# Latent-attention branch: head projections in pairs, the rotary parts of four heads in one tile, and scores summed from two products

## The chip, the cores and the metric

The kernel runs on one core of a Trainium2 chip. The engines of the core work side by side and meet at semaphores: TensorE (PE; its loading of stationary weights is listed apart as PEld), VectorE (DVE), ScalarE (ACT), GpSimd (POOL) and SyncE (SP), which issues most transfers. The metric is the time of one execution on the device in microseconds (us); lower is better. Three runs of the kernel before gave a median of 3520.85 us (3520.58 to 3526.13).

## The reference, cut to what matters

Two blocks with three attention branches each are followed by further layers, over 512 tokens of width 1024. Only the latent branch (here "A") is touched by the change. It has 8 heads. A head's query has 64 plain dimensions and 32 that are turned by the rotary embedding; the 32 rotary dimensions of the key are shared by all heads:

```python
def mla_mixer(c_q, c_kv, k_rope, g_q, g_kv, w_uq, w_ukv):
    q = (rms_norm(c_q, g_q) @ w_uq).reshape(B, S, MLA_HEADS, MLA_NOPE_DIM + MLA_ROPE_DIM)
    kv = (rms_norm(c_kv, g_kv) @ w_ukv).reshape(B, S, MLA_HEADS, MLA_NOPE_DIM + MLA_V_DIM)
    q_nope = q[..., :MLA_NOPE_DIM]
    q_rope = apply_rope(q[..., MLA_NOPE_DIM:], cos[:, None], sin[:, None])
    k_nope, v = kv[..., :MLA_NOPE_DIM], kv[..., MLA_NOPE_DIM:]
    k_rope = apply_rope(k_rope, cos, sin)
    ...
        s = (jnp.einsum('bqhd,bkhd->bhqk', qn, k_nope) + jnp.einsum('bqhr,bkr->bhqk', qr, k_rope)) * scale
        p = jax.nn.softmax(s, axis=-1)
        return jnp.einsum('bhqk,bkhd->bqhd', p, v)
```

S is 512, the latent ranks are 256 (queries) and 128 (keys and values).

## The kernel before, in words

All activations lie feature-major: features on the 128 partitions, 512 tokens along the free dimension. A projection (`feature_major`) takes 128 columns of weights as the stationary operand and streams 512 tokens; every product is three matmuls of split operands (high by high, low by high, high by low; lines 2278 to 2280). The weights come through HBM as a packed stream of 532 units of 128x1024. SP loads a unit into a ring of three, ACT rounds it into `w_hi` (L1337), DVE takes the difference into `w_lo` (L1730), and PE waits for that before a unit's first use. `split_ahead` and `before` set at which place of the ACT and DVE programs the next unit is split: as soon as the slot of three units earlier is free by the program's order.

Per layer the attention goes through seven groups of four heads: C0, B0, B1, B2, A0, A1, C1. `n_dense` says how many projection steps a group has (A: 5). While PE does the first three of them, it also does what is left of the group before (`attend(..., m)`, m = 0, 1, 2), so that softmax latency is covered. A group's own main part then runs in steps of two heads and one tile of 128 queries ("pair"): V (values), S (scores), T (probabilities transposed by PE), O (output). T lags S by two pairs and O by three. A latent group has 8 pairs.

In a latent group before, each head has its own projection of keys `kA` (128 columns, of which DVE keeps 64: L2059) and of queries `qA` (96 columns, two ranks deep, evicted by ACT at L1357). The rotary part is turned over the whole 96-row tile of each head: PE multiplies by a signed permutation (`rotation`, L2431), DVE multiplies that by the sine (L1883), POOL multiplies the tile by the cosine (L1200), DVE adds (L1891). POOL also copies the shared rotary key `kr` under each head's key (L1233). A score is then one float32 matmul over 96 rows (L2488). DVE takes the negated row maximum (L1898), ACT the exponential (L1510). T is L2496 with evictions by DVE (L1996) and ACT (L1521); O is L2509 or L2519.

Two things run around the start of A0. The last part of B2 ends with `mix_dilations` on DVE (L1956 to L1970), which needs one exponential of ACT in its middle (L1526) and after which POOL does the mixing (L1244 to L1246). And ACT copies out `qA` of head 3 only behind that exponential. Around the start of A1, the outputs of B2 and A0 are transposed (`turned`, L2406) and split into halves: high by ACT (L1366), low by DVE (L1743).

PSUM has eight banks. During attention S, T, V and the projections go round six of them in the fixed order of the plan, O has the other two. `start_group` makes PE wait until the bank's last content has been read.

## Time and profile before

| what | value |
|---|---|
| median of three runs | 3520.85 us |
| profiled execution | 3523.32 us |
| its span, first to last instruction | 3521.2 us |
| mean granted TensorE clock | 0.981 |
| PE busy | 3416.2 us, 97% of the span |
| DVE busy | 1615.7 us, 46% |
| ACT busy | 1192.3 us, 34% |
| POOL busy | 357.4 us, 10% |

The span is what one execution took from its first to its last instruction. A busy share is an average over all stages. The granted clock is the share of full speed (2.4 GHz) at which TensorE was allowed to run; 0.5 is the lower level of 1.2 GHz. Matmuls overlap, so what one costs in a row of them is the distance between two starts and not its own duration. One float32 matmul shows up as two records, a 128-column transpose and an fp32r product as one.

### The profile page before, as it was taken

Reading aid. Unit: us, or ns where it says so; the run is one execution under the profiler, and the core shown is the slowest. Engines: PE = TensorE matmul, PEld = TensorE weight load, DVE = VectorE, ACT = ScalarE, POOL = GpSimd, SP = SyncE. Lnnn points to the kernel's source line nnn. Section 1 sums busy time; section 2 is a strip of 40 time slices with the busy share of each in tenths; the row PEclk is TensorE's granted clock in tenths of the full one; section 3 lists DMA queues with packets and bytes.
Section 4 is the critical chain, followed back from the end, with each engine's and each line's share of the span. In section 5 each row is a group of like instructions: output and inputs, shape, how many; then the busy total and the mean of one; then the engine's idle time right before and its main releaser. Section 6 shows DMA issues by size and latency. Waiting matters only on the chain.

```text
span 3521.2 us, 41468 instructions
## 1 busy us (share of the span) xinstructions
PE 3416.2 (97%) x17020; PEld 2828.2 (80%) x17020; DVE 1615.7 (46%) x2332; ACT 1192.3 (34%) x1936; POOL 357.4 (10%) x325
## 2 busy tenths in 40 slices
PE   7998999999999999999999999999999999999998
PEld 6786788788887767887888888888888887788887
DVE  4446444434344455444343454333533357764244
ACT  3333322322233333323322332222422236643222
POOL 2013000100011120000000010001300031130001
PEclk9999999999999999999999999999999999999999
DMA  4121122222222211222222222222222222222222
GB/s 148 43 84 36 41 90 96 90 96 98 99 96 75 73 48 36 70 97 90 96 96 96 96 99 79 89 81 78 75 99 94 98 78 72 86 89 93 94 99 74
DMA packets 82954, 296.51 MB, mean 84 GB/s; under 512 B 9584, under 2 KB 11856, under 8 KB 82640
## 3 DMA queue, kind: packets, MB, share of 16 engines
q1 hardware_dynamic: 80064, 284.89, 23.8%
q0 software_dynamic: 2704, 8.98, 0.8%
q8 instruction: 136, 2.23, 0.3%
q14 instruction: 50, 0.41, 0.0%
HBM read 290.66 MB, written 3.18 MB: 83 GB/s over the span
## 4 chain that ended last, share of the span: by engine, by line
PE 89%; DVE 5%; ACT 4%; issue 1%; POOL 1%; DMA 0%; SPq 0%; DVEq 0%; ACTq 0%; POOLq 0%
PE bank L2278 26%; PE bank L2280 26%; PE bank L2279 26%; PE bank L2519 3%; PE bank L2488 3%; PE bank L2496 2%; DVE w_lo L1730 1%; PE bank L2636 1%; ACT w_hi L1337 1%; ACT arena L1517 1%; PE bank L2431 1%; DVE arena L2188 1%; PE bank L2345 1%; PE bank L2624 0%; DVE h_lo L1832 0%
## 5 line engine op out<-in xcount | busy, mean ns | idle before, releaser
L1730 DVE TENSOR_TENSOR w_lo<-raw_ring,w_hi 128x1024 fp32r<-128x1024 f32 x532 | 679.2, 1277 | 1306.0 <-ACT w_hi L1337 1305.1
L2278 PE MATMUL bank<-h_hi,w_hi 128*128 128x512 f32 (+1 forms) x2752 | 1073.8, 390 | 46.2 <-DVE w_lo L1730 30.3
L2279 PE MATMUL bank<-h_lo,w_hi 128*128 128x512 f32 (+1 forms) x2752 | 1060.1, 385 | 0.0
L2280 PE MATMUL bank<-h_hi,w_lo 128*128 128x512 f32 (+1 forms) x2752 | 1059.5, 385 | 0.0
L1337 ACT ACTIVATE w_hi<-raw_ring 128x1024 fp32r<-128x1024 f32 x532 | 562.0, 1057 | 1134.1 <-PE bank L2280 1063.9
L2278 PEld LDWEIGHTS bank<-h_hi,w_hi 128*128 128x128 f32 x2752 | 523.3, 190 | 158.1 <-issue 37.6
L2280 PEld LDWEIGHTS bank<-h_hi,w_lo 128*128 128x128 f32 x2752 | 522.9, 190 | 103.6
L2279 PEld LDWEIGHTS bank<-h_lo,w_hi 128*128 128x128 f32 x2752 | 523.2, 190 | 102.8 <-issue 2.6
L2278 PE MATMUL bank<-act_hi,w_hi 128*128 128x512 f32 (+2 forms) x1352 | 516.0, 382 | 10.8 <-DVE act_lo L1743 7.7
L2279 PE MATMUL bank<-act_lo,w_hi 128*128 128x512 f32 (+2 forms) x1352 | 512.3, 379 | 0.0
L2280 PE MATMUL bank<-act_hi,w_lo 128*128 128x512 f32 (+2 forms) x1352 | 512.1, 379 | 0.0
L1357 ACT ACTIVATE arena<-bank 128x512 f32<-128x512 f32 (+2 forms) x252 | 146.4, 583 | 644.7 <-DVE bank L1777 435.6
L2278 PEld LDWEIGHTS bank<-act_hi,w_hi 128*128 128x128 f32 (+1 forms) x1352 | 254.1, 188 | 61.6 <-issue 8.2
L2280 PEld LDWEIGHTS bank<-act_hi,w_lo 128*128 128x128 f32 (+1 forms) x1352 | 254.3, 188 | 48.6
L2279 PEld LDWEIGHTS bank<-act_lo,w_hi 128*128 128x128 f32 (+1 forms) x1352 | 254.4, 188 | 47.6 <-issue 0.2
L1777 DVE TENSOR_TENSOR bank<-bank,rb 128x512 f32<-128x512 f32 x148 | 102.7, 695 | 169.7 <-PE bank L2280 168.5
L2278 PE MATMUL bank<-w_hi,h_hi 128*128 128x256 f32 x576 | 163.8, 284 | 0.0
L2280 PE MATMUL bank<-w_hi,h_lo 128*128 128x256 f32 x576 | 163.0, 283 | 0.0
L2279 PE MATMUL bank<-w_lo,h_hi 128*128 128x256 f32 x576 | 163.0, 283 | 0.0
L1120 POOL TENSOR_TENSOR arena<-arena 128x512 f32<-128x512 f32 x42 | 58.2, 1387 | 906.9 <-ACT arena L1376 906.0
L2488 PE MATMUL bank<-arena 64*128 64x128 f32 (+4 forms) x464 | 125.7, 520 | 14.7 <-DVE arena L1891 9.5
L2519 PEld LDWEIGHTS bank<-arena 128*128 128x128 f32 x928 | 115.5, 199 | 6.4 <-ACT arena L1521 3.2
(193 smaller groups left out, 2785.5 us busy)
## 6 DMA issues: line engine op xcount, KB each, us to landing
raw_ring<-weights SPq DMA_DIRECT2D x532, 512.0 KB, 3.3
arena<-rpb POOLq DMA_DIRECT2D x16, 320.0 KB, 4.5
xs<-x_t SPq DMA_DIRECT2D x4, 512.0 KB, 7.8
out_t<-xs SPq DMA_DIRECT2D x16, 128.0 KB, 1.8
arena<-block SPq DMA_DIRECT2D x1, 1024.0 KB, 12.0
arena<-o_nat POOLq DMA_DIRECT2D x2, 512.0 KB, 3.3
arena<-ret POOLq DMA_DIRECT2D x4, 256.0 KB, 3.0
o_nat<-arena POOLq DMA_DIRECT2D x2, 384.0 KB, 3.0
```

The costliest lines, as they stand in the source:

```text
L1120: ins = nc.gpsimd.tensor_tensor(tile(sq), tile(sq), tile(sq + k), ALU.add)
L1337: nc.scalar.activation(w_slot(w_hi, u), raw_slot(u), ACT.Copy).then_inc(w_hi_ready, 1)
L1357: nc.scalar.activation(dst, src, func, scale=scale).then_inc(gelu_freed if key[0] == "ly" else act_freed, 1)
L1517: nc.scalar.activation(probs[:, at], masked[:, at], ACT.Exp, scale=-1.0, bias=neg, accum_out=total).then_inc(probs_ready, 1)
L1730: nc.vector.tensor_tensor(w_slot(w_lo, u), raw_slot(u), f32(w_slot(w_hi, u)), ALU.subtract) \
L1777: nc.vector.tensor_tensor(b[:, :], b[:, :], rb[:, :], ALU.mult).then_inc(row_scaled, 1)
L2278: nc.tensor.matmul(out, lhs[0], rhs[0], start=first, stop=False)
L2279: nc.tensor.matmul(out, lhs[0], rhs[1], start=False, stop=False)
L2280: return nc.tensor.matmul(out, lhs[1], rhs[0], start=False, stop=last)
L2488: mm = nc.tensor.matmul(b[rows, at], q, k, start=True, stop=True)
L2496: mm = nc.tensor.transpose(tile_t(b, n), tile_t(tile(PB + u % PB_RING), n), c("ident"))
L2519: mm = nc.tensor.matmul(b[:, t * HEAD:(t + 1) * HEAD], tile_t(turned_probs, n), V[:, k0 + n, d], start=n == 0, stop=n == k1 - k0 - 1)
```

## The change

The weights are regrouped. For a group of four heads, `qr` is one projection whose 128 columns are the rotary parts of four heads; `kA` and `qA` are now projections of two heads each, 64 plain dimensions per head, side by side on 128 partitions. A latent group has 3 projection steps in place of 5. The rotary tile `Q[:, 2, :]` is turned once for all four heads (`n_rotated`). The rotary key's weight columns are repeated four times in the input projection, so that `kr` comes out on all 128 partitions, and POOL's copies fall away. A score is two float32 matmuls that accumulate in one bank: one over the head's 64 plain rows, one over its 32 rotary rows. The two heads of a pair take turns: plain, plain, rotary, rotary. The packed stream has 530 units.

```diff
-            c = cols(m * P, P) if m < 3 else cols(A_COLS - MLA_QK, MLA_QK)
+            c = cols(m * P, P) if m < 3 else cols(A_COLS - MLA_ROPE, MLA_ROPE) * GH
...
-            for i, h in enumerate(heads):
-                many(out, (l, "kA", g, i), ("w_ukv", l), range(1), cols(h * P, P))
-                many(out, (l, "qA", g, i), ("w_uq", l), range(2), cols(h * MLA_QK, MLA_QK))
+            many(out, (l, "qr", g), ("w_uq", l), range(2),
+                 [(h * MLA_QK + MLA_NOPE, (h + 1) * MLA_QK) for h in heads])
+            for i in range(2):
+                two = heads[2 * i:2 * i + 2]
+                many(out, (l, "kA", g, i), ("w_ukv", l), range(1), [(h * P, h * P + MLA_NOPE) for h in two])
+                many(out, (l, "qA", g, i), ("w_uq", l), range(2),
+                     [(h * MLA_QK, h * MLA_QK + MLA_NOPE) for h in two])
...
-    return 6 if turns_v(br, g) else 5
+    return 6 if turns_v(br, g) else 3 if br == "A" else 5
+def n_rotated(br):
+    return {"A": 1, "B": 4, "C": 0}[br]
...
-                pool.wait_ge(cos_done, nth_rope(l, "B", 2, 3))
-                wait_acc(pool, (l, "B", 2, "S", GH - 1))
-                for half in range(2):
-                    two = slice(2 * half, 2 * half + 2)
-                    one = kr[r, :].rearrange("p (o s) -> p o s", o=1).to_broadcast([MLA_ROPE, 2, S])
-                    nc.gpsimd.tensor_copy(K[r, two, :], one).then_inc(krope_done, 1)
-                    pool.wait_ge(krope_done, 2 * l + half + 1)
-                    for m in range(2 * half, 2 * half + 2):
-                        cosines("A", 0, m)
-                    pool.wait_ge(cos_done, nth_rope(l, "A", 0, 2 * half + 1))
+                cosines("A", 0, 0)
+                pool.wait_ge(cos_done, nth_rope(l, "A", 0, 0))
...
-                    before((l, "rot", "A", 0, LAG_O - 2))
+                    before((l, "qA", 0, 1))
...
-                        if br == "A" and m < GH:
-                            copy_out((l, "qA", g, m), Q[0:MLA_QK, m, :], rows=MLA_QK, scale=MLA_QK ** -0.5)
+                        if br == "A":
+                            copy_out((l, "qA", g, m - 1) if m else (l, "qr", g), Q[:, m - 1 if m else 2, :],
+                                     scale=MLA_QK ** -0.5)
...
-                            nc.vector.tensor_copy(K[0:MLA_NOPE, m, :], b[0:MLA_NOPE, :]).then_inc(dve_freed, 1)
+                            nc.vector.tensor_copy(K[:, m - 1, :], b[:, :]).then_inc(dve_freed, 1)
...
-                if br == "A":
-                    return slice(0, P), slice(0, S), tile_t(Q[0:MLA_QK, i, :], t), K[0:MLA_QK, i, :]
+                if br == "A" and n:
+                    r = slice(MLA_ROPE * i, MLA_ROPE * (i + 1))
+                    return slice(0, P), slice(0, S), tile_t(Q[r, 2, :], t), kr[r, :]
...
-                                pe.wait_ge(rope_done, nth_rope(l, br, g, i))
-                                pe.wait_ge(krope_done, 2 * l + 1 + i // 2)
+                                pe.wait_ge(rope_done, nth_rope(l, br, g, 0))
+                                pe.wait_ge(krope_sum, l + 1)
+                                wait_freed(pe, (l, "kA", g, i // 2))
+                                wait_freed(pe, (l, "qA", g, i // 2))
...
-                        parts = NT if strided(br, g) else 2 if (br, g, t) == ("B", 0, 0) else 1
+                        parts = NT if strided(br, g) else 2 if br == "A" or (br, g, t) == ("B", 0, 0) else 1
...
-                                mm = nc.tensor.matmul(b[rows, at], q, k, start=True, stop=True)
+                                mm = nc.tensor.matmul(b[rows, at], q, k, start=br != "A" or n == 0,
+                                                      stop=br != "A" or n == 1)
```

PE's program at the first two pairs of A0, before: the last two rotations, the values V, the scores of pair 0, V, the scores of pair 1 (a row is one matmul, banks numbered).

```order
L2431 MATMUL bank5<-arena,fixed_sb 96x512
L2431 MATMUL bank0<-arena,fixed_sb 96x512
...
L2280 MATMUL bank2<-w_hi,act_lo 128x256
L2488 MATMUL bank3<-arena 128x512
L2488 MATMUL bank4<-arena 128x512
L2278 MATMUL bank5<-w_hi,act_hi 128x256
...
L2280 MATMUL bank0<-w_hi,act_lo 128x256
L2488 MATMUL bank1<-arena 128x512
L2488 MATMUL bank2<-arena 128x512
```

The same place in the changed program, from the last output of B2 (L2508) on; `kr` marks the rotary part of a score.

```order
L2508 MATMUL bank6<-arena 128x64 x4
L2508 MATMUL bank7<-arena 128x64 x4
L2275 MATMUL bank1<-w_hi,act_hi 128x256
...
L2277 MATMUL bank2<-w_hi,act_lo 128x256
L2486 MATMUL bank3<-arena 128x512
L2486 MATMUL bank4<-arena 128x512
L2486 MATMUL bank3<-kr,arena 128x512
L2486 MATMUL bank4<-kr,arena 128x512
```

No rotation stands between the last outputs of B2 and the scores any more, and each score bank is written by two matmuls.

DVE's program at the same place, before: from the last outputs of B2 (L1939) through `mix_dilations` to the first row maximum of A0 (L1898).

```order
L1939 COPY arena<-bank7 128x4x64
L1956 TENSOR_TENSOR small<-small 128x16
...
L1970 TENSOR_TENSOR small<-small 128x16 x3
L2059 COPY arena<-bank3 64x512
L1730 TENSOR_TENSOR w_lo<-raw_ring,w_hi 128x1024
L1883 TENSOR_TENSOR cs<-bank5,arena 96x512
L1891 TENSOR_TENSOR arena<-arena,cs 96x512
L1883 TENSOR_TENSOR cs<-bank0,arena 96x512
L1891 TENSOR_TENSOR arena<-arena,cs 96x512 x2
L1898 TENSOR_REDUCE small<-bank3 128x1
```

The same in the changed program (L1938 are the outputs, L1955 to L1969 `mix_dilations`, L1890 the only rotary addition, L1897 the row maximum).

```order
L2057 COPY arena<-bank5 128x512
L1890 TENSOR_TENSOR arena<-arena,cs 128x512
L1938 COPY arena<-bank6 128x4x64
L1938 COPY arena<-bank7 128x4x64
L1955 TENSOR_TENSOR small<-small 128x16
...
L1969 TENSOR_TENSOR small<-small 128x16 x3
L1731 TENSOR_TENSOR w_lo<-raw_ring,w_hi 128x1024
L1897 TENSOR_REDUCE small<-bank3 128x1
```

The rotary addition has moved ahead of `mix_dilations`; behind it only one weight split is left before the first row maximum.

DVE's program at the start of A1 in the changed kernel: outputs of A0 (L1945), weight splits, low halves of the transposed outputs. Before, one split stood among the rotary work, and one before the last key copy.

```order
L1945 TENSOR_TENSOR arena<-bank7,small 128x4x64
L1731 TENSOR_TENSOR w_lo<-raw_ring,w_hi 128x1024 x2
L1744 TENSOR_TENSOR act_lo<-bank1,act_hi 128x512
L1744 TENSOR_TENSOR act_lo<-bank2,act_hi 128x512
L1744 TENSOR_TENSOR act_lo<-bank3,act_hi 128x512
L1744 TENSOR_TENSOR act_lo<-bank4,act_hi 128x512
```

The two splits now stand together, straight ahead of the four low halves.

## Rows read from the trace of the kernel before

**Rows 1.** The page: the chain that ended last, by engine.

```profile
PE 89%; DVE 5%; ACT 4%; issue 1%; POOL 1%; DMA 0%; SPq 0%; DVEq 0%; ACTq 0%; POOLq 0%
```

**Rows 2.** PE's waits: line, who released it, us in total, times, longest.

```profile
PE bank L2488 <- DVE arena L1891: 9.5, 2, 4.9
...
PE bank L2431 <- ACT arena L1357: 5.5, 4, 2.5
...
PE bank L2488 <- DVE act_lo L1743: 4.5, 4, 1.9
PE bank L2278 <- DVE cs L1883: 3.3, 4, 1.3
```

**Rows 3.** Stretches: start:end, length, busy times, PEclk, DMA share, GB/s.

```profile
287.24:295.71 8.47, 8.47 (x18) 4.35 (x19) 7.64 (x8) 3.42 (x10) 8.23 (x4) 0.69 0.03 10
344.15:353.18 9.03, 9.03 (x19) 4.53 (x19) 4.48 (x7) 3.66 (x10) 0.00 (x0) 0.65 0.14 59
...
628.00:636.00 8.00, 6.99 (x24) 5.62 (x25) 5.08 (x9) 3.26 (x6) 0.00 (x0) 0.79 0.18 65
```

**Rows 4.** PE groups kept apart by shape: count, busy us, mean ns.

```profile
L2488 PE MATMUL bank<-arena 96*128 96x512 f32 x128 | 69.6, 675 | 13.2 <-DVE arena L1891 9.5 <-DVE act_lo L1743 3.7
L2431 PE MATMUL bank<-arena,fixed_sb 96*96 96x512 f32 x32 | 16.5, 606 | 5.5 <-ACT arena L1357 5.5
```

**Rows 5.** Timeline of PE in a projection step of A0: start, us, operation.

```profile
270.10 0.48 PE L2278 MATMUL bank<-act_hi,w_hi 128*128 128x512 f32 x1
270.42 0.39 PE L2279 MATMUL bank<-act_lo,w_hi 128*128 128x512 f32 x1
...
272.27 1.02 PE L2431 MATMUL bank<-arena,fixed_sb 96*96 96x512 f32 x2
273.13 1.89 PE L2509 MATMUL bank<-arena 128*128 128x64 f32 x16
```

**Rows 6.** Timeline of PE in the main part of A0: S, then T.

```profile
300.92 1.94 PE L2488 MATMUL bank<-arena 96*128 96x512 f32 x4
302.69 1.04 PE L2496 MATMUL bank<-fixed_sb,arena 128*128 128x128 f32 x8
```

**Rows 7.** Timeline of PE in C0, where two heads' 64-row scores alternate.

```profile
93.86 0.70 PE L2488 MATMUL bank<-arena 64*128 64x256 f32 x4
94.49 0.87 PE L2496 MATMUL bank<-fixed_sb,arena 128*128 128x128 f32 x6
...
96.58 0.92 PE L2488 MATMUL bank<-arena 64*128 64x384 f32 x4
97.43 0.66 PE L2496 MATMUL bank<-fixed_sb,arena 128*128 128x128 f32 x4
```

**Rows 8.** Timeline of PE at A0's start: first projection, last rotations, scores, transposes.

```profile
260.99 0.50 PE L2278 MATMUL bank<-act_hi,w_hi 128*128 128x512 f32 x1
...
280.51 1.10 PE L2431 MATMUL bank<-arena,fixed_sb 96*96 96x512 f32 x2 [2.48 <-ACT arena L1357]
...
287.24 3.76 PE L2488 MATMUL bank<-arena 96*128 96x512 f32 x4 [4.91 <-DVE arena L1891]
...
295.71 1.04 PE L2496 MATMUL bank<-fixed_sb,arena 128*128 128x128 f32 x8
```

**Rows 9.** Timeline of DVE at A0's start.

```profile
277.76 0.15 DVE L1956 TENSOR_TENSOR small<-small 128x16 f32<-128x16 f32 x1
...
281.34 1.65 DVE L1970 TENSOR_TENSOR small<-small 128x16 f32<-128x16 f32 x3
```

**Rows 10.** Timeline of ACT at A0's start: the first copy of a query projection.

```profile
265.95 0.58 ACT L1357 ACTIVATE arena<-bank 96x512 f32<-96x512 f32 x1
```

**Rows 11.** Timeline of PE after a wait in the feed-forward part.

```profile
629.01 0.47 PE L2278 MATMUL bank<-act_hi,w_hi 128*128 128x512 f32 x1 [3.07 <-DVE act_lo L1743]
```

**Rows 12.** DVE at A1's start: low halves of the transposed outputs, and a weight split.

```profile
337.45 1.69 DVE L1730 TENSOR_TENSOR w_lo<-raw_ring,w_hi 128x1024 fp32r<-128x1024 f32 x1 [1.91 <-ACT w_hi L1337]
...
342.73 2.47 DVE L1743 TENSOR_TENSOR act_lo<-bank,act_hi 128x512 fp32r<-128x512 f32 x4
```

More of the change, by code:

```diff
@@ L676, in tables @@
     ca, sa = rope(MLA_ROPE)
-    cos_a = np.ones((P, S), f)
-    sin_a = np.zeros((P, S), f)
-    cos_a[MLA_NOPE:MLA_QK] = np.tile(ca, (2, 1))
-    sin_a[MLA_NOPE:MLA_QK] = np.tile(sa, (2, 1))
+    cos_a, sin_a = np.tile(ca, (2 * GH, 1)), np.tile(sa, (2 * GH, 1))
     rot_b = rotation((0, HEAD), HEAD // 2, P)
-    rot_a = rotation((MLA_NOPE,), MLA_ROPE // 2, P)
+    rot_a = rotation(range(0, P, MLA_ROPE), MLA_ROPE // 2, P)
     q, k = np.arange(P)[:, None], np.arange(2 * P)[None, :]
@@ L961, in wait_probs, with turning @@
                 eng.wait_ge(probs_ready, nth_probs(l, br, g, u))
+        def turning(br, m):
+            return Q[:, 2, :] if br == "A" else Q[:, m, :] if m < 2 else K[:, m - 2, :]
         def vt_tile(br, g, f):
@@ L987, in nth_rope @@
         def nth_rope(l, br, g, m):
-            return l * 20 + (4 * g if br == "B" else 12 + 4 * g) + m + 1
+            return l * 14 + (4 * g if br == "B" else 12 + g) + m + 1
         row_order = []
@@ L1247, in _ @@
                 pool.wait_ge(mixed_b, l + 1)
-                for m in range(4):
-                    cosines("A", 1, m)
-                pool.wait_ge(cos_done, nth_rope(l, "A", 1, 3))
+                cosines("A", 1, 0)
+                pool.wait_ge(cos_done, nth_rope(l, "A", 1, 0))
                 wait_acc(pool, (l, "yt", "B", 2, 1))
@@ L1875, in rotate @@
             def rotate(l, br, g, m):
-                rows = MLA_QK if br == "A" else P
-                if m < 4:
+                if m < n_rotated(br):
                     key = (l, "rot", br, g, m)
@@ L2426, in rotation @@
                 key = (l, "rot", br, g, m)
-                rows = MLA_QK if br == "A" else P
-                tl = Q[0:rows, m, :] if br == "A" or m < 2 else K[0:rows, m - 2, :]
-                wait_freed(pe, (l, "qA", g, m) if br == "A" else (l, "qk", br, g, m))
+                wait_freed(pe, (l, "qr", g) if br == "A" else (l, "qk", br, g, m))
                 b = start_group(key)
-                nc.tensor.matmul(b[0:rows, :], c("rot_a" if br == "A" else "rot_b")[0:rows, 0:rows], tl, start=True,
-                                 stop=True).then_inc(acc_ready, 1)
+                nc.tensor.matmul(b[:, :], c("rot_a" if br == "A" else "rot_b"), turning(br, m), start=True, stop=True) \
+                    .then_inc(acc_ready, 1)
             def turned(l, group):
@@ L2569, in _ @@
                             norm_sum("q", l, SQC, 2)
-                            r = slice(MLA_NOPE, MLA_QK)
                             wait_freed(pe, (l, "cin", 3))
                             b = start_group((l, "krot"))
-                            nc.tensor.matmul(b[r, :], c("rot_a")[r, r], tile(KRAW)[r, :], start=True, stop=True) \
+                            nc.tensor.matmul(b[:, :], c("rot_a"), tile(KRAW), start=True, stop=True) \
                                 .then_inc(acc_ready, 1)
```

55 lines of the change are left out of this document (25 added, 30 removed).

## The prediction

> **What bounds the kernel now.** I read the chain of waits first: PE is 89% of what ended last [rows 1], so an instruction taken from PE's row shortens the time unless PE then waits. Second, PE's waits by releaser: in the two layers' latent groups PE waits 9.5 us for the rotary additions before the first scores of A0, 5.5 us for ACT's copies before rotations, 3.3 us for DVE's reading of a rotation's bank, and 3.7 us (of the 4.5) for low halves before the scores of A1 [rows 2, 4]. That is 22.0 us. Third, stretches by granted clock: after the wait at A0 the clock is 0.69 over 8.47 us, after those at A1 0.65 over 9.03 us [rows 3]; the missing shares are 0.31 x 8.47 = 2.6 and 0.35 x 9.03 = 3.2 us, and taking layer 1 alike, 11.6 us for both layers. So 33.6 us go to waits and half clock around the starts of latent groups; all else there is PE work at full speed. Last, the timelines, for what each PE operation takes from start to start.
>
> **Projections.** A step of nine products starts at 270.10 and the next operation at 272.27 [rows 5]: 2.17 us, of which the first takes 0.32 and the others 0.23 each. A group had four such steps, 8.68 us. Now it has 6, 9 and 9 products: 24 x 0.231 + 3 x 0.09 = 5.8 us. That is 2.86 us less per group, 11.4 us for four groups (two per layer, two layers). That the tiles are 128 columns wide instead of 96 costs nothing: stationary width does not show in the distance (0.23 both for `kA` and `qA`). The wider fourth input projection likewise.
>
> **Rotations.** One takes 272.27 to 273.13, 0.86 us [rows 5]. 32 records at half a matmul each are 16 rotations [rows 4]; 4 are left: -12 x 0.86 = -10.3 us. The four rotations of the shared key stay one float32 matmul of 512 columns each.
>
> **Scores.** A pair of 96-row scores takes 300.92 to 302.69, 1.77 us [rows 6]; 128 records are 32 pairs [rows 4]. Heads of 64 rows lie on different halves of the array. In C0 two of them with 256 columns take 0.63 us together, with 384 columns 0.85 us [rows 7]. One float32 matmul of 384 columns would by the 512-column rotation take 0.65 alone, so the two run side by side, with something fixed on top. The line through both points gives 0.22 us per 128 columns and 0.19 fixed: 1.07 us for the plain parts of a pair. The rotary parts lie on two different quarters of the array; no row of before shows such a pair. Bounds: side by side with nothing fixed 0.86 (one rotation), one after the other 1.77. I take 1.07, since the nearest row is that of C0. Pair: 2.14 us, +0.37, and 32 times that is +11.8 us.
>
> The Trainium skill (TensorEngine Tiling (Array Packing), Key Properties) says that changing the tiling mode drains TensorE; per pair the new order has one such change more (64 to 32 rows). By the row of C0 the 0.19 fixed is all that entering and leaving such a pair costs, and 2.14 counts it twice already [rows 7]. If by that rule a third 0.19 came on top, it would be 6 us in all, and the time 3506.
>
> PE work together: -11.4 - 10.3 + 11.8 = -9.9 us.
>
> **The start of A0.** ACT is busy with B2's exponentials until 265.95 and copies the first query tile then [rows 10]; the first rotation waits for that, before and now. So up to 270.10 nothing moves. Then come one projection step (2.17), B2's last outputs (1.7, a little under the 1.89 of their row [rows 5]) and V (0.75, estimated as six products of 256 columns at 0.12): the scores of A0 can start at 274.7, since POOL's cosine and DVE's addition are long done. Before, they started at 287.24 [rows 8]. What is late next is DVE: `mix_dilations` takes 277.76 to 281.34 + 1.65 = 283.0, 5.2 us [rows 9], now from about 275.0 to 280.2, and behind it a weight split of up to 1.69 [rows 12] stands ahead of the first row maximum. Two maxima and two exponentials (about 0.7 and 0.9 each, overlapping) free the banks of pair 0 at 284.3. PE has done pairs 0 and 1 by 279.8 and waits some 4.5 us for a bank. T starts at 286.5 instead of 295.71 [rows 8]: 9.2 us sooner, of which 4.35 is work. The other 4.9 us are waits and clock. I take back 2.2 us for a new fall of the clock: a 3.07 us wait elsewhere [rows 11] cost 0.21 x 8 = 1.7 us [rows 3], the 4.91 us wait here 2.6. Left: 2.7 us per layer.
>
> **The start of A1.** The wait for low halves stays, because two weight splits now stand ahead of them. From the end of A0's last outputs DVE needs 1.1 us for scaling, 2.6 for two splits and 1.2 for the first two low halves (four take 2.47 [rows 12]), so the scores' banks are free at 4.9; PE arrives at 2.9 (transposes 1.75, a wait of 0.4 for the outputs, V 0.75) and waits 2.0. Waits of 2.4 us against 3.5 (half of 3.3 + 3.7 [rows 2, 4]), and I halve the clock's 3.2: 2.7 us saved per layer.
>
> POOL loses 4 broadcasts and 12 cosines; nobody waits for POOL here, since the mixing ends well before its transposes. The stream has two units fewer and its cuts fall in the same places again behind each A1, so nothing moves later. The rotary key on 128 partitions instead of 32 changes no duration. All this at nothing; if a unit came late, one wait of 1 to 2 us.
>
> **Sum.** -9.9 - 2 x (2.7 + 2.7) = -20.7 us. On the profiled execution 3523.3 gives 3502.6; the median of before stands 2.5 us lower, so 3500.
>
> **Rivals.**
> - *The waits give nothing back.* DVE behind `mix_dilations` and at A1 is as late as before and the clock falls as long. For it: DVE's order [rows 9, 12], against it: 12.5 us of head start at A0. Only the work is left: 3511.
> - *More is given back.* The clock stays up (then 2 x 3.8 us more) and the rotary pair has nothing fixed (0.86: 6.7 us more). For it: the waits are split up. Against it: the wait in rows 11 did bring the clock down. Time: 3486.
> - *Slower: the score matmuls of a pair don't run side by side.* The place is the main part, all 32 pairs. With rotary parts one after the other a pair takes 1.07 + 1.77 = 2.84 us, +34 us in place of +11.8, and the time is 3522; with both parts in a row 3.54 us, +57 us, 3545. It decides from 1.77 + (21.7 + 10.8)/32 = 2.79 us a pair. Against it stand the rows of C0 [rows 7]; for it, that none shows 32-row tiles.
>
> **How the numbers follow.** My forecast 0.54, nothing given back 0.18, more given back 0.20, slower by serial scores 0.08. The range reaches from the third case to just above the second: 3485 to 3514. What can be told from no change is 0.2%, 7 us. Faster by that: the first and third case and most of the second, 0.87. Within: the rest of the second and the 3522 case, 0.07. Slower 0.06.
>
> **What would show it.** In the changed profile: four records of a pair's plain scores and four of its rotary scores, and T 2.14 us after the first. Over 2.3 us means a mode change or a serial part. Projection steps 1.5 and 2.17 us. At A0 no wait of over 1 us ahead of the first scores, but one of 3 to 5 us before those of pair 2, released by ACT. At A1 a wait of about 2 us released by a low half. Clock of about 0.7 over 3 to 7 us behind each of these. Wrong would be: T of A0 less than 5 us earlier with respect to the first projection of the group, DVE or ACT releasing PE in every pair of the main part, or a longer time in the layers that are not touched.

## The result, and the profile after

The changed kernel took 3484.31 us (median of 4 runs, 3483.23 to 3486.74), beside 3523.49 us for the kernel before on the same chip (4 runs, 3520.58 to 3538.14): a ratio of 0.9882, 95% interval 0.9853 to 0.9910. It is 39 us faster. The forecast was 3500 with a range from 3485; the direction was right, the gain was nearly twice as large as forecast, and the time lies just below the range.

| | before | after |
|---|---|---|
| span of the profiled execution | 3521.2 us | 3482.5 us |
| mean granted clock | 0.981 | 0.987 |
| PE busy | 3416.2 us | 3391.5 us |
| DVE busy | 1615.7 us | 1570.4 us |
| POOL busy | 357.4 us | 332.7 us |

PE's waits by releaser, answering to [rows 2] (line, who released it, us in total, times, longest):

```profile
PE bank L2486 <- DVE act_lo L1744: 4.3, 4, 1.7
...
PE bank L2486 <- ACT arena L1510: 2.1, 2, 1.1
PE bank L2426 <- ACT arena L1357: 2.1, 2, 1.0
```

Of 22.0 us of waits in the latent groups, 7.7 us are left: 2.1, 2.1 and 3.5 (of the 4.3; the other 0.8 stands at C1, as before). Both waits for the rotary work at the first scores of A0 are gone.

PE's start of A0, answering to [rows 8] (start, us, operation, idle before and releaser):

```profile
258.16 0.50 PE L2275 MATMUL bank<-act_hi,w_hi 128*128 128x512 f32 x1
...
263.75 1.13 PE L2426 MATMUL bank<-arena,fixed_sb 128*128 128x512 f32 x2 [1.03 <-ACT arena L1357]
...
272.04 1.13 PE L2486 MATMUL bank<-arena 64*128 64x512 f32 x4
273.10 1.13 PE L2486 MATMUL bank<-kr,arena 32*128 32x512 f32 x4
...
278.32 1.13 PE L2486 MATMUL bank<-arena 64*128 64x512 f32 x4 [1.07 <-ACT arena L1510]
...
280.44 1.09 PE L2495 MATMUL bank<-fixed_sb,arena 128*128 128x128 f32 x8
```

From the first projection to the first T it took 34.7 us before and now 22.3 us: 12.4 us less, where 9.2 were forecast. The wait before pair 2 was to be 4.5 us and is 1.07.

DVE over the same time, answering to [rows 9]:

```profile
271.73 0.17 DVE L1955 TENSOR_TENSOR small<-small 128x16 f32<-128x16 f32 x1
...
272.13 0.59 DVE L1958 TENSOR_TENSOR small<-small 128x16 f32<-128x16 f32 x3
...
274.37 0.59 DVE L1969 TENSOR_TENSOR small<-small 128x16 f32<-128x16 f32 x3
274.88 1.22 DVE L1731 TENSOR_TENSOR w_lo<-raw_ring,w_hi 128x1024 fp32r<-128x1024 f32 x1
276.01 2.56 DVE L1897 TENSOR_REDUCE small<-bank 128x1 f32<-128x512 f32 x4
```

`mix_dilations` now takes 3.2 us and not 5.2: the last three small operations take 0.59 us, where they took 1.65 [rows 9], and the three from 272.13 on take 0.59, where they took 1.54. What stood beside it before is on POOL. In the kernel before two of the four cosines of A0 run there:

```profile
278.16 1.54 DVE L1959 TENSOR_TENSOR small<-small 128x16 f32<-128x16 f32 x3
278.18 1.28 POOL L1200 TENSOR_TENSOR arena<-arena 96x512 f32<-96x512 f32 x1 [1.55 <-PE bank L2431]
281.69 1.27 POOL L1200 TENSOR_TENSOR arena<-arena 96x512 f32<-96x512 f32 x1 [2.23 <-PE bank L2431]
```

Taken singly, one small operation began 0.19 us behind the first of these cosines and one 0.07 us behind the second. They took 1.12 and 1.24 us, all others but the reciprocal 0.15 to 0.18, and each ended 0.03 us behind its cosine. Now one cosine is left, at 264.96, and nothing of POOL stands beside the mixing on DVE.

The clock in stretches behind the waits, answering to [rows 3] and [rows 11] (length, busy times of PE, PEld, DVE, ACT, POOL, granted clock, DMA share, GB/s):

```profile
60.00:72.00 12.00, 12.00 (x69) 10.18 (x68) 4.81 (x6) 2.53 (x4) 7.54 (x8) 1.00 0.52 182
278.00:286.00 8.00, 7.68 (x46) 4.51 (x47) 4.34 (x7) 5.53 (x18) 7.77 (x4) 1.00 0.07 27
323.70:331.00 7.30, 7.30 (x31) 2.62 (x31) 3.63 (x6) 3.33 (x10) 0.00 (x0) 1.00 0.55 223
609.00:617.00 8.00, 7.93 (x35) 6.59 (x36) 5.96 (x9) 2.95 (x5) 0.00 (x0) 1.00 0.10 31
```

Behind the waits of A0 (1.07 us) and A1 (1.75 us) the clock stays at its upper level of 2.4 GHz, in layer 1 as well. Before, it was 0.69 and 0.65 there. The last stretch lies behind a wait of 3.07 us as in [rows 11]; here the clock stays up, where it was 0.79 before. The first stretch is the start of the kernel, where the clock of the kernel before is lower:

```profile
60.00:72.00 12.00, 12.00 (x46) 8.93 (x45) 3.20 (x4) 1.47 (x3) 6.87 (x8) 0.72 0.53 191
```

PE in the main part of A0, answering to [rows 6]:

```profile
286.34 1.13 PE L2486 MATMUL bank<-arena 64*128 64x512 f32 x4
287.39 1.13 PE L2486 MATMUL bank<-kr,arena 32*128 32x512 f32 x4
288.45 1.09 PE L2495 MATMUL bank<-fixed_sb,arena 128*128 128x128 f32 x8
289.38 1.90 PE L2518 MATMUL bank<-arena 128*128 128x64 f32 x16
291.21 1.13 PE L2486 MATMUL bank<-arena 64*128 64x512 f32 x4
```

S to T takes 2.11 us (forecast 2.14). But the whole step, S to S, takes 4.88 us, against 4.38 before (300.92 to 305.30). T to O went from 0.88 to 0.93 and O to S from 1.73 to 1.83. The step costs 0.50 us more, not 0.37. Only the last five of a group's eight pairs stand in such a step.

Where the 38.7 us of the span came from can be read by landmarks that both traces have: the wait for the first softmax statistics in C0 (91.25, now 88.00), the first rotation of A0 (266.58, now 263.75), and the first scores of C1 (418.99, now 399.33); in layer 1 the difference grows from 22.4 to 39.0 between the last two. So the two latent parts gave 16.8 and 16.6 us, 33.4 together, and all the rest of the kernel 5.3, of which 3.25 at its very start.

### The profile page after: what moved, and what is told of

Its sections match the earlier page's. It is cut to its first block, busy times and chain, and to the rows that moved or that the text cites. A ratio compares the mean times of both kernels' runs of the same rounds, so it can differ in the third digit from the quotient of the medians.

```text
span 3482.5 us, 41528 instructions
## 1 busy us (share of the span) xinstructions
PE 3391.5 (97%) x17076; PEld 2807.3 (81%) x17076; DVE 1570.4 (45%) x2298; ACT 1186.6 (34%) x1930; POOL 332.7 (10%) x309
## 4 chain that ended last, share of the span: by engine, by line
PE 89%; DVE 4%; ACT 4%; issue 1%; POOL 1%; DMA 0%; SPq 0%; DVEq 0%; ACTq 0%; POOLq 0%
PE bank L2275 26%; PE bank L2277 26%; PE bank L2276 26%; PE bank L2518 3%; PE bank L2486 3%; PE bank L2495 2%; PE bank L2633 1%; DVE w_lo L1731 1%; ACT w_hi L1337 1%; ACT arena L1517 1%; DVE arena L2185 1%; PE bank L2426 1%; PE bank L2342 1%; PE bank L2621 0%; POOL xs L1141 0%
## 5 line engine op out<-in xcount | busy, mean ns | idle before, releaser
L2275 PE MATMUL bank<-act_hi,w_hi 128*128 128x512 f32 (+1 forms) x1336 | 508.7, 381 | 10.8 <-DVE act_lo L1744 7.7
L2277 PE MATMUL bank<-act_hi,w_lo 128*128 128x512 f32 (+1 forms) x1336 | 505.4, 378 | 0.0
L2276 PE MATMUL bank<-act_lo,w_hi 128*128 128x512 f32 (+1 forms) x1336 | 505.1, 378 | 0.0
L1357 ACT ACTIVATE arena<-bank 128x512 f32<-128x512 f32 (+1 forms) x248 | 143.5, 583 | 629.7 <-DVE bank L1778 435.6
L2275 PEld LDWEIGHTS bank<-act_hi,w_hi 128*128 128x128 f32 x1336 | 251.8, 188 | 60.4 <-issue 8.2
L2277 PEld LDWEIGHTS bank<-act_hi,w_lo 128*128 128x128 f32 x1336 | 251.6, 188 | 47.1
L2276 PEld LDWEIGHTS bank<-act_lo,w_hi 128*128 128x128 f32 x1336 | 251.9, 189 | 46.1 <-issue 0.2
L2518 PE MATMUL bank<-arena 128*128 128x64 f32 x928 | 117.2, 278 | 2.0 <-ACT arena L1521 2.0
```

The lines of the kernel that those rows point to most:

```text
L1357: nc.scalar.activation(dst, src, func, scale=scale).then_inc(gelu_freed if key[0] == "ly" else act_freed, 1)
L2275: nc.tensor.matmul(out, lhs[0], rhs[0], start=first, stop=False)
L2276: nc.tensor.matmul(out, lhs[0], rhs[1], start=False, stop=False)
L2277: return nc.tensor.matmul(out, lhs[1], rhs[0], start=False, stop=last)
L2518: mm = nc.tensor.matmul(b[:, t * HEAD:(t + 1) * HEAD], tile_t(turned_probs, n), V[:, k0 + n, d], start=n == 0, stop=n == k1 - k0 - 1)
```

## The experiments

Two questions had the most weight: why so little of the waits and of the half clock came back, and why a step of the main part costs more than its two score steps. The theory: with the rotary work gone the starts of A0 and A1 keep only short waits, DVE's mixing is short because POOL is idle beside it, and short waits don't bring the clock down. The rivals were that the clock stayed up by luck, and that the gain came from elsewhere.

**One rotation.** The kernel before, with one rotation for each latent group: three of four heads keep their rotary part unturned. Projections, scores and the order stay.

```diff
-    return has_rope(br) and 0 < m < 5
+    return has_rope(br) and 0 < m < (2 if br == "A" else 5)
...
-                if m < 4:
+                if m < (1 if br == "A" else 4):
                     key = (l, "rot", br, g, m)
...
-                                pe.wait_ge(rope_done, nth_rope(l, br, g, i))
+                                pe.wait_ge(rope_done, nth_rope(l, br, g, 0))
+                                wait_freed(pe, (l, "kA", g, i))
+                                wait_freed(pe, (l, "qA", g, i))
```

> The kernel before with one rotation per latent group instead of four: heads 1 to 3 of each group keep their rotary part unturned (left out of the computation), projections, 96-row scores and POOL's two key copies stay. Theory 1 (the gain came from the rotations, in work and in the chain behind them): 12 rotations x 0.86 = 10.3 us of work go, and most of the 22.0 us of waits and 11.6 us of half clock at the starts of A0 and A1 go too, so 3523.5 - 30 to -36, about 3490, and PE's wait before A0's first scores falls from 4.9 us to under 2. Theory 2 (the waits went because scores, projections and steps were regrouped): only the 10.3 us go, 3513, and the waits before A0's scores stay at 3 us or more.

Measured: 3500.78 us (3485.06 to 3502.71), ratio 0.9922 (0.9899 to 0.9945), beside 3523.43 us before: 23 us less. Of these 10.3 are the rotations' own time. The time lies between the two theories (3490 and 3513). PE's waits at A0 became (the operations with a wait, of layer 0):

```profile
283.51 0.39 PE L2277 MATMUL bank<-w_hi,act_hi 128*128 128x256 f32 x1 [0.84 <-DVE arena L2058]
287.93 1.95 PE L2489 MATMUL bank<-arena 96*128 96x512 f32 x4 [1.72 <-ACT arena L1509]
```

The 4.9 us wait is gone with the rotations, as the first theory has it, and `mix_dilations` takes 3.2 us here too. Of the 22.0 us of waits 9.1 are left. The clock behind the waits of A0 stays at 1.00 in layer 0, but it fell elsewhere in this execution (0.61 over 7.8 us at 618, 0.57 over 16 us at 2839). One run of four took 3485 us, with a mean granted clock of 0.986 against 0.981 to 0.982 in the others. So the turning of the heads alone gives over half of the gain, and most of the waits.

**POOL busy beside the mixing.** The changed kernel, with four multiplications on POOL while DVE runs `mix_dilations`.

```diff
                 pool.wait_ge(cos_done, nth_rope(l, "A", 0, 0))
+                wait_acc(pool, (l, "B", 2, "O", GH - 1))
+                for _ in range(4):
+                    then(nc.gpsimd.tensor_tensor(K[:, 3, :], c("cos_a"), c("cos_a"), ALU.mult))
```

> The changed kernel with four more multiplications on POOL (tables into a tile nobody reads, 1.3 us each), started when B2's last output is done, so that they lie beside mix_dilations on DVE. Theory 1 (mix_dilations took 5.2 us before because POOL's cosines ran beside it, and 3.2 us now because they don't): it takes 5 us or more again, the row maxima start 2 us later and PE's wait before pair 2 of A0 grows from 1.07 to about 3 us; 2 x 2 = +4 us, or up to +9 if the clock falls then. Theory 2 (DVE's small steps took longer for another reason): mix_dilations stays at 3.2 us and the time at 3484 within 1 us.

Measured: 3500.61 us (six runs: four of 3497 to 3501, two of 3521 and 3524). All are above the changed kernel. DVE, POOL and PE of the profiled execution, one of the two long ones:

```profile
272.33 0.84 DVE L1958 TENSOR_TENSOR small<-small 128x16 f32<-128x16 f32 x1
...
273.42 2.05 DVE L1961 TENSOR_TENSOR small<-small 128x16 f32<-128x16 f32 x3
...
275.77 1.22 DVE L1967 TENSOR_TENSOR small<-small 128x16 f32<-128x16 f32 x3 [0.31 <-ACT small L1529]
...
277.73 0.59 DVE L1972 TENSOR_TENSOR small<-small 128x16 f32<-128x16 f32 x3
```

```profile
272.10 4.45 POOL L1241 TENSOR_TENSOR arena<-arena 128x512 f32<-128x512 f32 x4 [5.26 <-PE bank L2511]
```

```profile
277.40:338.80 61.40, 61.17 (x203) 38.58 (x204) 18.10 (x33) 16.89 (x42) 11.25 (x5) 0.50 0.03 9
338.80:353.00 14.20, 13.43 (x95) 11.83 (x94) 7.27 (x13) 6.42 (x11) 2.94 (x4) 1.00 0.03 5
...
1307.10:1315.00 7.90, 7.87 (x20) 3.11 (x20) 2.18 (x4) 3.81 (x11) 7.66 (x4) 0.50 0.07 26
```

The mixing took 6.0 us in place of 3.2. Beside each of the four POOL multiplications one small operation took 0.81 to 0.90 us, where it takes 0.17 us alone. It began some 0.2 us behind the multiplication and ended 0.03 us behind it. This answers the first part: 5.2 us in the forecast was the mixing with POOL's cosines, which the change removes. The longer mixing also held back an exponential of ACT and, behind it, a weight split and the copies of the values, so PE waited 1.63 us ahead of pair 1 and, in layer 1, 1.97 us more ahead of pair 2. The clock went to half behind the wait of 1.63 us in both layers, once for 10 us and once for 61 us, the whole main part of A0. The expectation had the direction and the longer mixing right, but neither the place of the wait (3 us before pair 2; in layer 0 it was 0.23 us) nor its price: 4 to 9 us were expected and 16 measured. The Trainium skill (GPSIMD Engine Reference, Specifications) says that GpSimd shares its SBUF interfaces with VectorE, with contention for instructions that have two SBUF inputs. The small operations here have two, and the trace agrees: 0.81 to 0.90 against 0.17 us.

**PE held for the mixing.** The same question from the other side: no POOL work, one wait made long.

```diff
                     if kind == "V":
+                        if (br, g, j) == ("A", 0, 0):
+                            pe.wait_ge(lse_alpha, l + 1)
```

> The changed kernel, with TensorE held before the first values of A0 until the vector engine is through with mixing the dilations: by the trace of the changed kernel from 271.15 to about 274.96, 3.8 us of idle in each layer, and the wait of 1.07 us before pair 2 of A0 gone, since the maxima are no longer late. By idle time alone 2 x (3.8 - 1.1) = 5.4 us more than the changed kernel, 3489. Theory (a wait of this length ahead of the scores takes the clock down as well, as the one of 4.91 us did in the kernel before): half clock for 3 us or more at A0 in at least one layer, 3492 to 3496, and up to 3520 in runs where it stays low through the main part, as behind POOL's multiplications. Rival (what took the clock down behind POOL's multiplications was two waits close together, or something POOL did): no half clock at A0 in either layer, 3487 to 3490.

Measured: 3496.14 us (3495.46 to 3496.79), ratio 0.9919 (0.9891 to 0.9947), beside 3525.12 us for the kernel before. That is 12 us more than the changed kernel, which wasn't run beside it. PE, and the clock behind the wait in either layer:

```profile
275.26 0.58 PE L2275 MATMUL bank<-w_hi,act_hi 128*128 128x256 f32 x1 [3.66 <-DVE small L1969]
```

```profile
275.20:284.00 8.80, 8.74 (x24) 4.22 (x24) 2.42 (x4) 2.76 (x8) 8.43 (x4) 0.51 0.18 62
1280.20:1290.00 9.80, 9.72 (x37) 4.06 (x37) 3.75 (x6) 4.05 (x12) 9.32 (x5) 0.83 0.16 55
```

The wait of 3.66 us brings the clock down in both layers, with POOL idle. By the clock record it is at half for 10.2 us in layer 0 and for 3.4 us twice in layer 1, at A0 and at A1. Idle time accounts for 2 x (3.66 - 1.07) = 5.2 us. Of the 17 us of half clock 1.7 lie inside the wait of layer 0 (from 273.6 on) and cost nothing; half of the other 15.3 is 7.7, so 12.9 in all, against 11.8 measured. So the rival that POOL or a double wait is needed falls. No run lay near 3520.

**Only the plain parts.** The changed kernel with the rotary products of the scores left out.

```diff
-                        parts = NT if strided(br, g) else 2 if br == "A" or (br, g, t) == ("B", 0, 0) else 1
+                        parts = NT if strided(br, g) else 2 if (br, g, t) == ("B", 0, 0) else 1
```

> The changed kernel without the rotary part of the latent scores (left out of the computation): one 64-row matmul per score. Theory 1 (plain and rotary parts each take 1.06 us a pair, and the change between 64, 32 and 128 rows costs some 0.15 us a pair more than the 96-row form did): a pair's cycle falls from 4.87 to 3.7 us, 32 x 1.15 = -37 us, about 3447. Theory 2 (the rotary part is cheap, most of the 0.49 us a pair more than before lies in leaving the full array at all): the cycle falls by 1.06 or less and transposes and outputs keep their longer distances (0.93 and 1.83); 3450 or more.

Measured: 3456.79 us (3455.17 to 3459.28), 27.5 us less than the changed kernel. The main part of A0:

```profile
284.06 1.13 PE L2486 MATMUL bank<-arena 64*128 64x512 f32 x4
285.12 1.09 PE L2494 MATMUL bank<-fixed_sb,arena 128*128 128x128 f32 x8
286.04 1.90 PE L2517 MATMUL bank<-arena 128*128 128x64 f32 x16
287.87 1.13 PE L2486 MATMUL bank<-arena 64*128 64x512 f32 x4
```

A step takes 3.82 us, so the rotary step is worth 4.88 - 3.82 = 1.06 us, 33.9 us for 32 pairs. The time fell by less, since DVE and ACT are now late: PE waits 2.56 us before pair 2 in place of 1.07, and the clock is at half for 3.4 us behind it in both layers. The useful part is the rest of the step: T to O (0.92) and O to S (1.83) are as long as in the changed kernel, without any 32-row tile. The 0.15 us that my price lacked belongs to having 64-row tiles in the step at all, and not to the further change from 64 to 32 rows. That is the sign that the second theory named; the first, with its 3447 us, falls.

**Head by head.** The changed kernel with both parts of one head ahead of those of the other.

```diff
-                        for n in range(parts):
-                            for b, (u, i, t) in zip(outs, two):
+                        each = list(zip(outs, two))
+                        for n, (b, (u, i, t)) in ([(n, x) for x in each for n in range(parts)] if br == "A" else
+                                                  [(n, x) for n in range(parts) for x in each]):
```

> The changed kernel with the four score matmuls of a pair in another order: plain and rotary part of the first head, then plain and rotary part of the second. Nothing else differs. Theory (two score matmuls run side by side only when neighbours in the order lie on different rows and have the same tile height): a pair costs four matmuls one after the other, each 0.86 (a rotation of the same 512 columns) to 1.06 us in place of two steps of 1.06: 3.4 to 4.2 in place of 2.12 us, 32 pairs: 42 to 68 us more than the changed kernel, 3526 to 3552. Rival (the matmuls find each other whatever their order, since rows 64 to 127 are free while the first head's rotary part runs on rows 0 to 31): the rotary part of the first head and the plain part of the second run together, about 3.2 us, 34 us more, 3518. Rival (they never ran side by side; a matmul with fewer rows is shorter by itself): no change, 3484.

Measured: 3720.24 us (3716.04 to 3728.85), ratio 1.0558 (1.0536 to 1.0581): 237 us more than the changed kernel beside it, where the theory gave 42 to 68. The first pair of A0, and stretches over the main parts:

```profile
271.11 1.12 PE L2487 MATMUL bank<-arena 64*128 64x512 f32 x2
272.16 1.12 PE L2487 MATMUL bank<-kr,arena 32*128 32x512 f32 x2
273.21 1.12 PE L2487 MATMUL bank<-arena 64*128 64x512 f32 x2
274.26 1.12 PE L2487 MATMUL bank<-kr,arena 32*128 32x512 f32 x2
275.31 0.58 PE L2275 MATMUL bank<-w_hi,act_hi 128*128 128x256 f32 x1
```

```profile
275.00:364.00 89.00, 89.00 (x201) 44.85 (x201) 16.41 (x27) 16.22 (x41) 10.41 (x5) 0.50 0.02 6
364.00:381.00 17.00, 15.25 (x106) 13.18 (x105) 9.63 (x16) 7.21 (x13) 2.95 (x4) 1.00 0.12 41
381.00:477.00 96.00, 96.00 (x208) 47.10 (x208) 16.72 (x27) 15.93 (x40) 0.00 (x0) 0.50 0.04 14
```

At full clock a pair takes 4.20 us, four matmuls one after the other at 1.05 each, as the theory has it; that is 66.6 us for 32 pairs. The rotary part of the first head (rows 0 to 31) and the plain part of the second (rows 64 to 127) lie on different rows and in different banks, and still one starts 1.05 us behind the other (272.16 to 273.21), so the rival that they find each other in any order falls. The rest of the time is the clock. PE has not waited since 263, yet the clock is at half from 275.3 through the whole main part, rises during the projections (1.00 in the second row) and falls again in the next main part, there behind a wait of 1.75 us. The four main parts spend 358 us at half clock by the clock record; half of it is 179 us. With the 66.6 that makes 246 us. It is some 12 too many, since a pair at half clock takes 8.00 us (276.89 to 284.89) and not twice 4.20. I had not foreseen this term. The order of two matmuls decides here between 3484 and 3720 us.

**The wide rotary key alone.** The kernel before, with the key's columns repeated four times.

```diff
-cols(A_COLS - MLA_QK, MLA_QK)
+cols(A_COLS - MLA_ROPE, MLA_ROPE) * GH
...
-nc.gpsimd.tensor_tensor(kr[r, :], tile(KT1)[r, :], tile(KT2)[r, :], ALU.add)
+nc.gpsimd.tensor_tensor(kr[:, :], tile(KT1), tile(KT2), ALU.add)
```

> The kernel before with the rotary key made four times by the projection (128 columns, its turning on 128 partitions); heads as before. The changed kernel is 3.2 us ahead already at C0, where the clock of before is 0.62 to 0.82 from 60 to 72 us. Theory 1 (the 32x32 matmul of the key's rotation let the clock fall, the full one does not): the clock stays at 1.0 there, C0's first transposes start near 88.0 instead of 91.25, time -3 us. Theory 2 (that the clock fell there is chance of when it is looked at): no clear difference, and the clock may fall there or not in the timed runs.

Measured: 3517.01 us (9 runs, 3512.74 to 3522.06), ratio 0.9979 (0.9969 to 0.9989). The start of the kernel, where the change has the same clock of 1.00 and the kernel before 0.72:

```profile
60.00:72.00 12.00, 12.00 (x69) 10.17 (x68) 5.68 (x7) 2.53 (x4) 7.11 (x7) 1.00 0.50 171
```

PE in the kernel before, where the clock falls at 63.8 by the clock record:

```profile
63.31 1.47 PE L2573 MATMUL bank<-arena,fixed_sb 32*32 32x512 f32 x2
```

An edit that I had priced at nothing is worth 6 us in the median. In the profiled execution C0's first wait ends at 87.14 us against 91.25, 4 us sooner, most of it by the clock (6.8 us at half, which cost 3.4). The fall begins in the middle of the key's rotation over 32 rows. The other kernel with the narrow key, the one with one rotation, has it at the same place (64.5, inside its 32-row rotation). The nine profiled executions with the wide key have none before 148 us. So the fall goes with the narrow key, and chance is an unlikely reading. Which of the two edits on PE keeps the clock up (128 columns in place of 96 in the projection, or 128 rows in place of 32 in the rotation) is not shown. At A0 and A1 this kernel waits as the one before does (4.92 us at A0), and the clock falls in all four places again.

**The changed kernel again, and two versions with shorter waits.** The first is the changed kernel itself. The second moves two of DVE's weight splits at A1 behind the low halves. The third also takes DVE's split ahead of the first maxima away, and puts the rotation behind T and O of the group before.

```diff
-                    lo(key, part(act_lo, i), group(key)[:, :], part(act_hi, i))
+                    lo(key, part(act_lo, i), group(key, step=late)[:, :], part(act_hi, i))
```

```diff
-                        if not turns_v(br, g):
+                        if not turns_v(br, g) and br != "A":
                             before((l, "v", br, g, v_tiles(j)[-1]))
...
-                        if rotates(br, m):
+                        if br != "A" and rotates(br, m):
                             rotation(l, br, g, m - 1)
                         if j and m < LAG_O:
                             attend(l, *GROUPS[j - 1], m)
+                        if br == "A" and rotates(br, m):
+                            rotation(l, br, g, m - 1)
```

> The changed kernel once more, as the base for the two kernels that are run beside it. If the 39 us are a property of the kernel, its median is 3484 again, within 4 us, and most of its runs lie within 5 us of each other. If the clock's standing at full speed behind the waits at the starts of A0 and A1 was luck of the first runs, some runs lie 10 to 37 us higher, as 2 of 6 did for the kernel with multiplications on POOL.

Measured: 3483.43 us (3481.47 to 3491.72), ratio 0.9888 (0.9869 to 0.9907). The 39 us are the kernel's and not luck. In its profile too the clock stays at full speed behind the waits of A0 and A1.

> The changed kernel, with DVE's two weight splits at the start of A1 behind the four low halves instead of ahead of them. Theory (what is late there is DVE's order): the low halves that free the banks of A1's first scores come 1.7 us sooner or more, PE's wait of 1.75 us falls to under 0.2, the first maxima come 1 us later and bring a wait of 0 to 0.3 us before pair 2; 2 x 1.6 = 3.2 us less than the changed kernel, 3481. Rival (PE waits for ACT's high halves or for the bank order anyway): the wait stays over 1 us and the time within 1 us. Rival (the shorter wait moves a fall of the clock): the wait goes and the time changes by 3 us or more in either direction beyond that.

Measured: 3478.22 us (3474.39 to 3479.53), ratio 0.9865 (0.9847 to 0.9883), 5.2 us less than the changed kernel beside it. DVE and PE at A1:

```profile
319.40 2.48 DVE L1744 TENSOR_TENSOR act_lo<-bank,act_hi 128x512 fp32r<-128x512 f32 x4 [0.51 <-ACT act_hi L1366]
321.80 2.35 DVE L1731 TENSOR_TENSOR w_lo<-raw_ring,w_hi 128x1024 fp32r<-128x1024 f32 x2
```

```profile
326.38 1.13 PE L2486 MATMUL bank<-arena 64*128 64x512 f32 x4 [0.34 <-ACT arena L1510]
```

The wait of 1.75 us is gone and one of 0.34 has come before pair 2, close to what the theory has: 2.8 us in two layers. The rest of the 5.2 lies within the spread of the runs.

> The changed kernel with three moves: the late splits of the kernel before in this list; no weight split on DVE ahead of the first maxima of a latent group (it comes with the third pair); the one rotation of a latent group behind the last transposes and outputs of the group before, in place of ahead of them. Theory: the waits of 1.03 us (first rotation of A0), 1.07 us (pair 2 of A0) and 1.75 us (A1) all go, 3.9 us a layer, of which the ones at A0 are 2.1 to 2.1: 7.0 to 7.7 us less than the changed kernel in all, 3477. Rival (what a removed wait gives is asked back by the next): ACT's exponentials, 0.67 us behind each maximum, or the weight piece that was moved are late in their turn, a wait of 0.5 us or more stands in the main part of A0 or A1, and the gain is under 4 us.

Measured: 3478.42 us (3473.88 to 3480.44), ratio 0.9867 (0.9851 to 0.9884): no gain over the version before it. The waits did go, save one of 0.68 us that moved to the transposes ahead of the rotation, and C1's scores start 1.5 us sooner (395.4 against 396.9). But in the profiled execution the clock fell at 606 us behind the 3.07 us wait of the feed-forward part, where it had stayed up in the other version:

```profile
606.00:614.00 8.00, 8.00 (x30) 6.41 (x29) 4.98 (x8) 1.47 (x2) 0.00 (x0) 0.79 0.00 0
```

So the time came near the expected 3477, but the gain over the changed kernel is 5.0 us and not 7.0 to 7.7, and the working was not met: neither theory names a place outside the latent groups. Both versions beat the changed kernel by 5 us, and which of the two is better these runs don't tell.

Waits at the starts of the latent groups, and how long the clock was at half in or behind them, from the profiled executions (us; layer 0 / layer 1):

| kernel | wait at A0 | half clock | wait at A1 | half clock |
|---|---|---|---|---|
| before | 2.5 + 4.9 / 2.5 + 4.6 | 6.8 / 10.2 | 1.3 + 1.9 | 6.8 / 6.8 |
| PE held | 3.66 / 3.66 | 10.2 / 3.4 | 1.75 | none / 3.4 |
| plain parts only | 0.56 + 2.56 / 0.56 + 2.55 | 3.4 / 3.4 | 1.75 | 3.4 / none |
| one rotation | 0.84 + 1.72 | none / 3.4 | 1.73 | 3.4 / none |
| changed, and again | 1.07 | none / none | 1.75 | none / none |

In this table each wait from 2.55 us up had a fall in it or behind it, those of 1.7 us had one sometimes, those of 1.07 us none. The two waits of 2.5 us of the kernel before stand ahead of the last rotation. In layer 0 the clock fell only in the wait of 4.9 us after it; in layer 1 it fell 1.3 us behind the one of 2.5 us, at 1296.0, when the next wait had not begun:

```profile
1296.00:1306.20 10.20, 5.60 (x15) 3.27 (x14) 10.10 (x9) 0.77 (x2) 9.80 (x5) 0.50 0.16 51
1301.43 3.75 PE L2488 MATMUL bank<-arena 96*128 96x512 f32 x4 [4.60 <-DVE arena L1891]
```

Of these 10.2 us at half clock PE was busy for 5.60, in layer 0 for 5.3 of 6.8. Half clock costs only where PE works, so both layers lost about the same: 2.8 and 2.6 us. The table holds for the latent groups. Behind the wait of 3.07 us in the feed-forward part the clock fell in the kernel before and in the one with three moves, and not in the changed kernel or the one with late splits.

## Why the prediction was wrong

The mechanism was right: 12 rotations and the products of the projections less, scores dearer, and PE bound throughout. The step that failed is the sum over the starts of A0 and A1, "-9.9 - 2 x (2.7 + 2.7)": the second term was 10.8 us and is 26 us. Within it, the wait before pair 2 of A0 was put at 4.5 us and is 1.07, and the half clock that was to follow the waits did not come.

| term | forecast | measured |
|---|---|---|
| projections | -11.4 | -11.4 (a step of six products takes 1.48 us, of nine 2.15) |
| rotations | -10.3 | -10.3 (12 x 0.86; one left takes 0.86, or 0.97 behind the wait at A0, as the first did before with 0.94) |
| scores with T and O | +11.8 | +14.1 (four groups of 3.53) |
| waits at A0 and A1 | } -10.8 | -14.3 (22.0 to 7.7) |
| half clock there | } together | -11.6 (by the 33.6 us account) |
| the rest of the kernel | 0 | -5.3 |
| sum | -20.7 | -38.8; span -38.7 |

- *The wait before pair 2 of A0 (4.5 us forecast, 1.07 measured).* I moved `mix_dilations` with the duration that it had, 5.2 us, though [rows 9] show three 128x16 operations at 1.65 us and a single one at 0.15. The operations that slowed it down, POOL's cosines, were among those that the change removes, and I had noted their removal as worth nothing ("nobody waits for POOL here"). The run with POOL busy shows it: 6.0 us against 3.2. This is 2.0 of the 3.4 us. Another 0.6 are the weight split behind it: I took "up to 1.69" from [rows 12], and from the end of the mixing to the first maximum it is 1.05 us (274.96 to 276.01). That split, too, stood beside two cosines of POOL (336.78 to 340.26); whether they slowed it was not tried. The last 0.8 are small: the mixing began 0.4 us sooner with respect to the first projection, PE came 0.3 us later, and the rest is rounding.
- *The clock behind the short waits.* I gave back 2.2 us at A0 and half of 3.2 us at A1 for new falls. This followed from the wait that didn't come: at 4.5 us it would have fallen, as it did at 3.66 in the run with PE held; at 1.07 it didn't, in any of four places. At A1 the wait was forecast well (2.0, measured 1.75), and the clock differed from execution to execution there: no fall in the changed kernel, one in one of two layers with PE held, with plain parts only and with one rotation. What decides it is not shown, so at A1 the forecast missed by something that no row could give.
- *The scores.* 2.14 forecast and 2.11 measured for S to T, so both parts run side by side, each with about 0.2 us fixed. What was missing is 0.05 us ahead of O and 0.10 ahead of the next S, where a pair has them. From the first T of A0 to the projections behind it takes 25.27 us in place of 22.70 (280.44 to 305.71, before 295.71 to 318.41), and the three pairs ahead of the first T take 0.96 more, waits taken off, than in the kernel with one rotation. That is 3.53 us a group against the 2.95 forecast, 2.3 us in all. I took the price of a row-tiled step from S to T in [rows 7] and not over the whole step, S to S. The Trainium skill (TensorEngine Tiling (Array Packing), Key Properties) says that changing the mode drains TensorE. The trace agrees that the mode has a price outside the score step, 0.15 us a pair, but the run with plain parts alone shows that it doesn't grow with the second change of mode, and the estimate of 6 us for that change falls away.
- *The rest.* 5.3 us came from places that the change doesn't touch but for the wider key, 3.25 of them from the clock at 60 to 72 us. The layers after that drift by 1 to 3 us either way with the clock. I had put this at nothing, as "or a longer time in the layers that are not touched" shows; a shorter one wasn't considered.
- *The rivals.* "More is given back" came nearest at 3486, right in that the clock stays up, wrong in that the rotary pair had no fixed part. Its time is near by luck: the 6.7 us that it took for the rotary pair did not come, and in their place stand the shorter wait at A0 (2 x 3.4 us) and the 5.3 us of the rest, which it did not have. The slower rival rested on score matmuls that run one after the other. Its price of 34 to 57 us was too low: the run head by head cost 237 us, since half clock over the main parts is part of that case.

The sum comes within 0.1 us of the span, closer than the single terms are known. Taking layer 1's half clock like layer 0's was right: 11.6 us in all also by the clock record, with the time that PE waited taken out.

## What to carry to other kernels

Before you move a stretch of another engine in time, ask which of its operations were slow and what ran beside them; if the change removes that too, take the duration from a row where it ran alone. A wait of TensorE has two prices, itself and the clock behind it, and the second goes with the first: when a long wait becomes short, take both away. Price a row-tiled matmul step over the whole cycle in which it stands, and keep matmuls of the same tile height on different rows next to each other in the program. An extra that you expect to cost nothing, as the wide key, is worth a run of its own.

## What the runs showed of the hardware

- The clock can fall and stay at half without any wait. With the score matmuls of a pair one after the other it was 0.50 over 89 us of uninterrupted PE work (busy 89.00), with the last wait 12 us before, and over 96 us more behind a wait of 1.75 us, and 1.00 in the projections between them. With two of them side by side, the same matmuls ran at 1.00 in the changed kernel.
- Once down, it could stay down in a main part that otherwise holds full speed: 61 us in the run with POOL busy, in which PE was busy 61.17 of 61.40 us. In layer 1 of the same execution it rose after 10 us.
- A 128x16 operation with two SBUF inputs on VectorE took 0.17 us alone. Begun 0.07 to 0.26 us behind a GpSimd multiplication it ended 0.03 us behind it, in all twelve cases of two executions (the kernel before and POOL busy, both layers): 0.81 to 0.90 us beside multiplications of 1.04 to 1.07 us, 1.12 and 1.24 us beside cosines of 1.27 and 1.28 us.
- Two 64-row float32 matmuls of 512 columns take 1.06 us side by side and one alone 1.05; the same holds for 32 rows. A 32-row and a 64-row one on different rows did not run side by side (1.05 us from start to start).
- The clock fell inside the key's rotation over 32 rows in both profiled executions that had it (63.8 and 64.5 us), and in none of the nine with 128 rows and a wider projection.
